# Two tuned blocks of a transformer on one core: the work around scan, mLSTM, linear attention, weight slots and warm-up put in another order, and x fetched by two queues

## The reference

```python
def first_block(x, mem, ...):
    x = x + token_mixer(rmsnorm(x, norm_mix), w_in, b_in, ...)   # hgrn2_scan + mlstm_scan, both directions, @ w_out
    x = x + cross_attention(rmsnorm(x, norm_xattn), rmsnorm(mem, norm_mem), w_xq, w_xkv, w_xo)
    x = x + squared_relu_mlp(rmsnorm(x, norm_mlp), w_up, w_down)
    return rmsnorm(x, norm_final)

def second_block(x, ...):
    proj = rmsnorm(h, norm_mix) @ w_in
    y_att = windowed_gqa(aq, ak, av, attn_sink) @ w_branch_attn
    y_gla = gla_branch(gq, gk, gv, gr, z_f, z_b, ...) @ w_branch_gla
    h = h + (sigmoid(g_att) * y_att + sigmoid(g_gla) * y_gla) @ w_out
    h = h + expert_choice_ffn(rmsnorm(h, norm_ffn), w_router, w_exp_gate, w_exp_up, w_exp_down)
    h = h + sigmoid(rmsnorm(h, norm_ple) @ w_ple_gate) * (p @ w_ple)
    return rmsnorm(h, norm_final)
```

## Time and profile before

| | us |
|---|---|
| median of 3 runs | 1871.67 |
| lowest, highest | 1871.23, 1877.39 |
| the profiled execution's own time | 1871.47 |
| its span in the profile | 1869.7 |
| TensorE busy | 1817.9 |
| GpSimd busy | 978.1 |
| VectorE busy | 782.6 |
| ScalarE busy | 549.4 |

### The profile page before, as it was taken

How to read it: one execution, slowest core, us unless ns; L and a number is a source line. 1 busy time by engine, 2 the same in 40 slices (tenths; PEclk the granted TensorE clock), 3 DMA queues, 4 the chain that set the end, 5 groups by cost and what they waited for, 6 DMA issues and landing times.

```text
span 1869.7 us, 22394 instructions
## 1 busy us (share of the span) xinstructions
PE 1817.9 (97%) x9105; PEld 1346.8 (72%) x9105; DVE 782.6 (42%) x1154; ACT 549.4 (29%) x1037; POOL 978.1 (52%) x547
## 2 busy tenths in 40 slices
PE   7998999999999999999999999999999999999998
PEld 6887888788888888888777888878744444433456
DVE  4375777734524301422676565433221222221234
ACT  5534557522422101211233444332230000000025
POOL 6499958467378878897565896437500000000022
PEclk9999999999999999999999999999999999999999
DMA  6231125223123222333322322114999999999991
GB/s 210 86 90 46 46 79 181 68 68 109 39 91 92 100 101 91 102 113 92 114 79 69 90 90 83 53 57 148 387 385 410 428 427 427 428 428 427 421 373 56
DMA packets 82918, 335.83 MB, mean 180 GB/s; under 512 B 6528, under 2 KB 8320, under 8 KB 67712
## 3 DMA queue, kind: packets, MB, share of 16 engines
q1 hardware_dynamic: 79296, 322.47, 46.1%
q10 hardware_dynamic: 3520, 11.93, 1.7%
HBM read 328.08 MB, written 6.29 MB: 179 GB/s over the span
## 4 chain that ended last, share of the span: by engine, by line
PE 80%; POOL 7%; DMA 5%; DVE 4%; ACT 2%; issue 1%; SPq 0%; ACTq 0%; DVEq 0%; POOLq 0%
PE bank L669 52%; PE bank L2168 13%; PE bank L2205 3%; DMA arena<-in_w_exp_up 3%; POOL arena L1007 2%; PE bank L2187 2%; DMA shared<-in_w_exp_up 2%; POOL arena L1003 2%; PE bank L690 1%; POOL shared_r L987 1%; PE bank L2322 1%; PE bank L1192 1%; PE bank L1829 1%; PE bank L1840 1%; PE bank L1206 1%
## 5 line engine op out<-in xcount | busy, mean ns | idle before, releaser
L669 PE MATMUL bank<-shared_r 128*128 128x512 f32 (+2 forms) x3036 | 699.0, 387 | 5.6 <-DVE shared_r L767 1.8
L669 PEld LDWEIGHTS bank<-shared_r 128*128 128x128 f32 x3036 | 554.2, 188 | 122.9 <-issue 9.3
L708 POOL TENSOR_TENSOR shared_r<-shared,small 128x1024 fp32r<-128x1024 f32 (+1 forms) x134 | 260.4, 1943 | 244.4 <-PE bank L669 243.8
L709 POOL TENSOR_TENSOR shared_r<-shared,shared_r 128x1024 fp32r<-128x1024 f32 (+1 forms) x134 | 327.2, 2442 | 10.5
L708 POOL TENSOR_TENSOR spare_r<-arena,small 128x1024 fp32r<-128x1024 f32 x2 | 3.8, 1892 | 468.5 <-DMA arena<-in_w_ple_gate 468.5
L2168 PE MATMUL bank<-arena 128*64 128x512 f32 x624 | 186.6, 596 | 0.8 <-ACT arena L2260 0.5
L2168 PE MATMUL bank<-shared,arena 128*64 128x512 f32 x592 | 181.4, 602 | 6.0 <-DMA shared<-in_w_exp_up 2.9
L669 PE MATMUL bank<-shared_r,arena_r 128*128 128x512 f32 x624 | 146.0, 393 | 0.0
L669 PEld LDWEIGHTS bank<-shared_r,arena_r 128*128 128x128 f32 x624 | 117.8, 190 | 24.2
L2168 PEld LDWEIGHTS bank<-shared,arena 128*64 128x64 f32 x592 | 58.6, 139 | 91.2 <-issue 91.2
L2168 PEld LDWEIGHTS bank<-arena 128*64 128x64 f32 x624 | 59.9, 138 | 56.8 <-issue 55.6
(11 more groups left out here) (483 smaller groups left out, 2600.8 us busy)
## 6 DMA issues: line engine op xcount, KB each, us to landing
shared<-in_w_in SPq DMA_DIRECT2D x80, 512.0 KB, 3.6
shared<-in_w_exp_up SPq DMA_DIRECT2D x11, 2048.0 KB, 25.5
arena<-in_w_exp_down SPq DMA_DIRECT2D x11, 2048.0 KB, 30.1
arena<-in_w_exp_gate SPq DMA_DIRECT2D x10, 2048.0 KB, 31.2
shared<-in_w_exp_gate SPq DMA_DIRECT2D x9, 2048.0 KB, 20.8
arena<-in_w_exp_up SPq DMA_DIRECT2D x9, 2048.0 KB, 23.7
shared<-in_w_up SPq DMA_DIRECT2D x32, 512.0 KB, 3.7
...
```

Of the source, the lines that this page charges most:

```text
L669: ins = pe.matmul(dst, W_, x_, start=first, stop=final)
L708: link(pool.tensor_tensor(hi, raw(p), small[:, 18:19].to_broadcast([P, hi.shape[1]]), ALU.add))
L709: pool.tensor_tensor(lo, raw(p), hi.bitcast(F32), ALU.subtract).then_inc(S_("w_split"), 1)
```

## The change

- **Start.** SP issues tiles one and three of x, ScalarE tiles two and four, ahead of everything else in its program. TensorE runs 18 matmuls of the identity by itself before its first wait for x.
- **Slots.** `proj_g` and `proj_v` join the stages with four slots.
- **Products.** The wait for a fresh K tile stands in front of its first matmul instead of in front of the part.
- **Scan.** The sums of the next unit's keys go from GpSimd to VectorE; the copy `pairs(u, 3)` goes ahead of them and of `query(u, 5)`; ScalarE makes `keys_of` behind the evictions; GpSimd splits at most one weight part per level and waits for the sums at the unit's end.
- **mLSTM.** Three of the four gating multiplications go ahead of the first head, the fourth behind its cells; the normalisation goes behind the second head's cells; two evictions of turned rows go from ahead of the last head's cells to between them.
- **Linear attention.** The squares of chunk 0 go behind the last evictions; the first turn comes after 8 instead of all 12 remaining groups of `proj_r`, the second after 5 instead of 8 groups of `ygla`.

```diff
--- before.py
+++ after.py
@@ -294,7 +294,7 @@
         else:
             eng.wait_ge(part_used, parts[p]["signal"])
 
-    wide = [p for a, b in (("proj_h", "proj_m"), ("down1", "proj_g"), ("gatt", "ygla")) for w in range(PB[a], PB[b]) for p in panels[w]["parts"]]
+    wide = [p for a, b in (("proj_h", "proj_m"), ("down1", "ygla")) for w in range(PB[a], PB[b]) for p in panels[w]["parts"]]
     between = [p for w in range(PB["xk"], PB["out1"]) for p in panels[w]["parts"]]
     scanned = [p for w in range(PB["proj_m"], PB["proj_m"] + 3) for p in panels[w]["parts"]][:11]
     split_at, slot_user, last_in = {}, {}, [None] * 4
@@ -408,6 +408,9 @@
             act.wait_ge(S_("first_sq"), j + 1)
             act.activation(var[:, 0, j:j + 1], mean8[:, 0, 0, j:j + 1], ACT.Sqrt, bias=eps_).then_inc(S_("first_sd"), 1)
 
+        x = A["x"].rearrange("a (j p) d -> p (a j) d", p=P)
+        for j in range(1, ST, 2):
+            act.dma_start(X[:, j, :], x[:, j, :]).then_inc(S_("x_in%d" % j), 16)
         act.wait_ge(S_("consts"), 1)
         act.activation(small[:, 19:20], eps_, ACT.Sqrt)
         square(0)
@@ -436,6 +439,7 @@
     def first_pe(pe):
 
         pe.wait_ge(S_("ident"), 1)
+        keep_busy(pe, BASE["norm_mix"] + KT - 1, 18)
         for j in range(ST):
             pe.wait_ge(S_("first_xs"), j + 1)
             for d in range(KT):
@@ -645,17 +649,16 @@
                 pe.wait_ge(raw_full[p % 4], 16 * (p // 4 + 1))
                 halves = [raw(p).rearrange("p (k n) -> p k n", k=part["kp"])]
                 pairs = ((0, 0),)
-            for kk in range(part["kp"] if ready is not None else 0):
-                if isinstance(ready, Hidden):
-                    pe.wait_ge(S_("ht_lo"), ready.first + part["k0"] + kk + 1)
-                else:
-                    bank_done(pe, ready[part["k0"] + kk])
             for g in range(panel["groups"]):
                 n = panel["base"] + g
                 opens = p == panel["parts"][0] and panel["opens"]
                 bank = bank_claim(pe, n) if opens else banks[BANK[n]]
                 for kk in range(part["kp"]):
                     k = part["k0"] + kk
+                    if g == 0 and isinstance(ready, Hidden):
+                        pe.wait_ge(S_("ht_lo"), ready.first + k + 1)
+                    elif g == 0 and ready is not None:
+                        bank_done(pe, ready[k])
                     for a, b in pairs:
                         if fm:
                             W_, x_ = halves[a][:, kk, g * P:(g + 1) * P], x[b][:, k, 0:toks]
@@ -934,8 +937,6 @@
                     act.activation(HKD[1], HKD[1], ACT.Exp).then_inc(S_("h_kd"), 1)
                     for d in range(2):
                         act.activation(EG_[2 * (u % 2) + d], CH[:, d, :, chunk_of(d, u), C], ACT.Exp)
-                elif l == 3 and u < ST - 1:
-                    keys_of(u + 1)
                 elif l == 5 and u:
                     if u >= 2:
                         bank_written(act, hg_bank["out", 1, u - 1])
@@ -943,6 +944,8 @@
                     c = chunk_of(1, u)
                     towards_end(HQD[1], hg_view(CH, 1, c), 1, c).then_inc(S_("h_eqd"), 1)
                 hg_evacuate(act, done, hg_seen(g))
+                if l == 3 and u < ST - 1:
+                    keys_of(u + 1)
                 split_hi(act, "proj_m", hi, min(14, hg_parts(hg_seen(g))))
             for d in range(2 if u < ST - 1 else 0):
                 n = hg_bank["keys", d, u]
@@ -1006,16 +1009,13 @@
                     one, two = (key, ref) if d else (ref, key)
                     ins = pool.tensor_tensor(hg_half(k, b, d), one, two, ALU.subtract)
                 ins.then_inc(S_("h_d"), 1)
-                hg_split_lo(pool, False, lo, min(14, hg_parts(hg_seen(g - 1))) if g else 1)
+                hg_split_lo(pool, False, lo, min(14, lo[0] + 1, hg_parts(hg_seen(g - 1))) if g else 1)
                 if l == 0 and u < ST - 1:
                     if u:
                         bank_written(pool, hg_bank["keys", 1, u - 1])
                     c = chunk_of(1, u)
                     pool.tensor_tensor(HKD[1], hg_view(CH, 1, c), NLK[:, 1, :, c * C:(c + 1) * C], ALU.subtract).then_inc(S_("h_w"), 1)
-                if l == 4 and u < ST - 1:
-                    if u:
-                        pool.wait_ge(S_("h_kd"), 2 * u - 1)
-                    keys_sum(pool, u + 1)
+                if l == NL - 1 and u < ST - 1:
                     pool.wait_ge(S_("h_w"), 2 * u + 3)
         hg_split_lo(pool, False, lo, 14)
         bank_written(pool, BASE["proj_m"] + 8)
@@ -1114,12 +1114,16 @@
             pairs(u, 2)
             for d in range(2 if u else 0):
                 state(d, u - 1)
+            pairs(u, 3)
             if u == 1:
                 dve.tensor_copy(FG[0:64, :], GZ[64:128, :]).then_inc(S_("fg"), 1)
             if u < ST - 1:
+                if u:
+                    dve.wait_ge(S_("h_kd"), 2 * u - 1)
+                dve.wait_ge(S_("h_w"), 2 * u + 2)
+                keys_sum(dve, u + 1)
                 key_both(u + 1)
             query(u, 5)
-            pairs(u, 3)
             query(u, 6)
             pairs(u, 4)
             for d in range(2 if u else 0):
@@ -1389,6 +1393,10 @@
         conv_taps(dve, link, 1, (0, 1, 3, 4))
         scan_half = MIX[:, :, 0:512].rearrange("p c (h x) -> p c h x", h=H)
         dve.wait_ge(S_("cols"), 1)
+        for t in range(ST - 1):
+            if t == 2:
+                dve.wait_ge(S_("conv"), 5)
+            dve.tensor_tensor(MIX[:, t, 0:512], MIX[:, t, 0:512], GATE[:, t, 0:512], ALU.mult)
 
         def near(h):
 
@@ -1424,10 +1432,10 @@
             if h + 1 < H:
                 bank_done(dve, score(h, ST - 1))
                 near(h + 1)
-            if h == H - 1:
-                for d in range(2):
-                    evac_lo(dve, BASE["turn_a"] + d, XTS[:, 1, d, :], XTS[:, 0, d, :], mix_gain(d))
             for t in range(ST):
+                if h == H - 1 and t == 2:
+                    for d in range(2):
+                        evac_lo(dve, BASE["turn_a"] + d, XTS[:, 1, d, :], XTS[:, 0, d, :], mix_gain(d))
                 n = cell_out(h, t)
                 bank = bank_take(dve, n)
                 den = bank[:, :].rearrange("p (d x) -> p d x", d=2)[:, :, C]
@@ -1438,18 +1446,14 @@
                 o = MIX[:, t, 512 + h * P:512 + (h + 1) * P]
                 link(dve.tensor_scalar(o, bank[:, 0:C], sm_a[:, 0:1], None, ALU.mult))
                 release_own(dve, dve.scalar_tensor_tensor(o, bank[:, 256:256 + C], sm_a[:, 1:2], o, ALU.mult, ALU.add), n)
-                if h == 0:
-                    if t == ST - 1:
-                        dve.wait_ge(S_("scan_sq"), 1)
-                    ins = dve.tensor_tensor(MIX[:, t, 0:512], MIX[:, t, 0:512], GATE[:, t, 0:512], ALU.mult)
-                if h == 1:
-                    if t == 0:
-                        dve.wait_ge(S_("sd_part"), 2)
-                        link(dve.reciprocal(heads_of(head_r, 0), heads_of(head_ss, 0)))
+            if h == 0:
+                dve.wait_ge(S_("scan_sq"), 1)
+                link(dve.tensor_tensor(MIX[:, ST - 1, 0:512], MIX[:, ST - 1, 0:512], GATE[:, ST - 1, 0:512], ALU.mult))
+            if h == 1:
+                dve.wait_ge(S_("sd_part"), 2)
+                link(dve.reciprocal(heads_of(head_r, 0), heads_of(head_ss, 0)))
+                for t in range(ST):
                     ins = dve.tensor_tensor(scan_half[:, t], scan_half[:, t], heads_of(head_r, 0)[:, t].unsqueeze(2).to_broadcast([P, H, C]), ALU.mult)
-            if h == 0:
-                link(ins)
-            if h == 1:
                 ins.then_inc(S_("mix_a"), 1)
         for d in range(2, 4):
             evac_lo(dve, BASE["turn_a"] + d, XTS[:, 1, d, :], XTS[:, 0, d, :], mix_gain(d))
@@ -1928,9 +1932,9 @@
             if u == ST - 1:
                 link(gla_squares(act, 1))
                 link(gla_squares(act, 2))
-        link(gla_squares(act, 0))
         gla_evacuate(act, done, gla_first + gla_each * ST)
         assert done[0] == 12
+        link(gla_squares(act, 0))
         gla_squares(act, ST - 1).then_inc(S_("gla_sq"), 1)
         act.wait_ge(S_("gla_ms"), 1)
         act.activation(head_ss[:, 0:16], head_ss[:, 0:16], ACT.Sqrt).then_inc(S_("gla_sd"), 1)
@@ -2526,12 +2530,12 @@
         product(pe, PB["yatt"], [OTS[:, b] for b in range(2)], fm=True)
         steps = chain(*(product_steps(pe, PB["proj_r"] + i, XB, fm=i < 2) for i in range(4)))
         gla_pe(pe, steps)
-        run_steps(steps, 13)
+        run_steps(steps, 8)
         gla_turn(pe, 0)
         for _ in steps:
             pass
         steps = chain(*(product_steps(pe, PB["ygla"] + 2 * h + i, [GTS[:, b, 4 * h:4 * h + 4] for b in range(2)], fm=True, ready=eight("turn_gla")[4 * h:]) for h in range(2) for i in range(2)))
-        run_steps(steps, 8)
+        run_steps(steps, 5)
         gla_turn(pe, 1)
         for _ in steps:
             pass
@@ -3118,7 +3122,7 @@
     @block.sync
```

(2 more changed lines are left out.)

## The result

The changed kernel takes 1891.46 us (median of 4 runs, 1890.58 to 1892.86) against 1873.57 for the kernel before on the same chip: ratio 1.0094, 95% interval 1.0074 to 1.0115. It is slower by 18 us. I had forecast 1857.1 us, inside 1851 to 1866.5, and gave slower a chance of 0.05.

What follows compares the result with a forecast made beforehand. TensorE, busy 97% of the span, was taken as the bound. Gains of 1.2 (start), 8 (scan), 2.0 (mLSTM), 0 (attention) and 3.2 (linear attention) sum to 14.4: 1871.5 - 14.4 = 1857.1 us, range 1851 to 1866.5.

Steps and rivals of the forecast that it cites:

- The start: Kernel start: warm-up matmuls raise TensorE's clock early and the first product begins sooner; 1.2 us gained, range 0 to 1.9.
- The 0.9 us that the later tile was to cost: Kernel start: if tiles one and two of x share the DMA engines, everything behind is 0.9 us late.
- The scan: First scan, about 120 to 260 us: moved key sums and an earlier copy remove TensorE's gaps; 8 us gained, range 3 to 11.
- Rival (a): Scan: gives only 3 to 4 us, since VectorE takes GpSimd's place as pacer; 1861.5 us, chance 0.17.
- mLSTM: mLSTM, 310 to 370 us: gaps of 0.58 and 0.92 us and some smaller stalls go; 2.0 us gained, range 0.5 to 3.
- the fourth and the normalisation go behind the cells: mLSTM: VectorE's fourth gating multiplication and the normalisation move behind the cells, with no cost put on it.
- Attention: Entry to windowed attention, 930 to 945 us: the 1.33 us wait goes, a later one becomes 1.9; 0, range -0.5 to 1.3.
- those don't come sooner: Entry to attention: VectorE's rotated rows come no sooner, so TensorE's 0.53 us wait for them becomes 1.9.
- Linear attention: End of linear attention, 1228 to 1268 us: waits of 0.57, 1.78 and 0.35 us go; 3.2 us gained, range 1.5 to 3.4.
- (b): Start: two queues bring x later and the start gives nothing or loses a little; 1858.3 us, chance 0.10.
- (c): Kernel end: the experts' weight stream is not paced by TensorE and absorbs everything; 1871 us, chance 0.04.
- (d): Scan: sums on VectorE meet GpSimd's levels and take the worst duration each time; slower, 1880 us, chance 0.05.

Runs made afterwards that it cites:

- u_x: The changed kernel with all four tiles of x issued by SyncE's queue again, warm-up kept: 1890.88 us, ratio 1.0090 to the kernel before.
- b_key: The changed kernel without its collisions, plus GpSimd's second level of the first unit waiting until VectorE has added the first keys: 1865.69 us, against 1863.00 without that wait.
- u_norm: The changed kernel with the mLSTM normalisation of the second head group back in the loop over the four tiles: 1883.10 us, ratio 1.0049 to the kernel before.
- n_wait: The changed kernel with one added wait: GpSimd's last split of xv waits until the four mLSTM normalisations are done: 1880.56 us, ratio 1.0044 to the kernel before.
- w_roped: The changed kernel with GpSimd splitting two parts of proj_g, then waiting for VectorE's rope before the other two: 1879.89 us, ratio 1.0028 to the kernel before.

## Why the prediction was wrong, step by step

- **The start: right.** 1.2 forecast, 1.22 measured; first square at 5.66, matmuls 0.11 us apart before the transposes, first product between 14.0 and 14.9. The 0.9 us that the later tile was to cost, it did not: GpSimd's split ended last with one queue as with two (u_x).
- **The scan: mis-sized.** Eight were forecast, 0.6 came, and 3 once pairs(u, 4) stood ahead of query(u, 6). Two steps failed. I let GpSimd and TensorE run ahead by nearly all of the 8.6 us that GpSimd sheds, with the sums as the only new cost; the sums were nearly as I put them (8.2 us for 7.1), but GpSimd's levels grew by 2.9 and the additions of keys by 1.3. The spread in the earlier trace rows, 693 to 2844 ns for one shape, was the sign of it, and I took its median. And I followed the copy that moved ahead of the sums, but not pairs(u, 4), which moved behind a query. Rival (a) gave the scan 3 to 4, which is what it brings with that order put right; its reason, VectorE in GpSimd's place, holds for the wait of 2.81, while b_key shows GpSimd pacing unit one where VectorE does not. What each step is worth was measured only for the order, 2.6 us.
- **mLSTM: the failed step is "the fourth and the normalisation go behind the cells", costed at nothing.** The two gaps did go, and 2.3 us were gained up to 345, as forecast (2.0). The four operations, moved together behind the loop, took 10.05 us beside GpSimd in place of 3.57: 9.8 lost, 8.4 given back by u_norm, 9.4 to 10.9 by n_wait.
- **Attention: the mechanism was half seen.** I wrote that the wait of 1.33 goes, that the rotated rows don't come sooner and the wait becomes 1.9. The 1.33 went, but the wait became 9.9: 11.6 us lost. The failed step is "those don't come sooner", as if they could not come later. I took the rope's duration as fixed, while 8 of its 11.4 us before were already GpSimd's (w_roped: 3.3 us). The slots that let GpSimd split ahead made it 19.25.
- **Linear attention: half right.** The first turn gained 2.9, the 0.57 and 1.78 us and a little more. The second was given three groups to cover VectorE's eight operations at 3.25 us; they became 10.25, and 5.3 were lost.
- **The rivals.** (b) was right that the tiles come later and wrong that the start gains nothing. (c) is out: the end kept what the stages lost. (d) had the mechanism, VectorE meeting GpSimd at the worst duration, but put it at the sums alone, where pairs cost 2.2 to 3.5 and not 5.7; it decided where I did not look. It should have stood for every moved VectorE operation, and for a GpSimd made busier.

In short, I priced each instruction where it stood, and the change altered what ran beside it.
